# Gated DeltaNet and windowed attention, one core: the inverse's two upper levels by smaller blocks, and four steps put elsewhere

## The chip, the cores and the metric

One NeuronCore of a Trainium2 chip runs the whole program in one launch. Its engines are TensorE (PE; its weight loads are shown as PEld), VectorE (DVE), ScalarE (ACT), GpSimd (POOL) and SyncE (SP), which issues the weight loads from HBM. The metric is the device time of one execution in microseconds (us).

## The reference, cut to what matters

A prompt of 256 tokens and a decode batch of 8 go through a gated DeltaNet layer and a windowed attention layer, each followed by a SwiGLU block. The change touches the DeltaNet layer alone, where each head needs, for each chunk of tokens, the inverse of a lower triangular matrix:

```
a_mat = jnp.where(strict, jnp.einsum('bhnid,bhnjd->bhnij', kb, k) * decay, 0.0)
t_mat = lax.linalg.triangular_solve(a_mat + eye, jnp.broadcast_to(eye, a_mat.shape),
                                    left_side=True, lower=True)
u = t_mat @ (v * beta[..., None])
...
o = rms_norm(o, gnorm) * jax.nn.silu(z)
y = o.astype(h.dtype).reshape(B, L, DN_VAL_DIM) @ w_out
```

The kernel works with chunks of 128 tokens (the reference with 64), so each inverse is 128x128.

## The kernel before, in words

**Weights.** Every projection is done in chunks of 128x1024 weights. A chunk is loaded by SP, ACT rounds it (`split_hi`, line 460, `w_hi`), DVE makes the rest (`split_lo`, line 467, `w_lo`), and PE then runs 24 matmuls of 128x264 on it (`tiles`, lines 479 to 481: w_hi by h_hi, w_hi by h_lo, w_lo by h_hi). There are four buffers of raw weights and two of the split ones, so ACT may split chunk c only once PE is through with chunk c-2.

**Turns.** The DeltaNet layer's 32 heads come in 16 groups of two. `turn(g, G, last)` projects group g (12 chunks, j = 0 to 11) while group G = g-1 goes through its delta rule in 24 steps, n = 0 to 23: PE does step 2j, half of chunk j, step 2j+1, and the other half. So a step of PE comes once in some 2.2 us. ACT, DVE and POOL have their own parts of each step, in a hand written order around the splits. `first_turn` projects group 0 with no delta rule beside it; the last turn (g is None) takes the first 12 chunks of the output projection in place of a projection's.

**The inverse.** Four 128x128 matrices (two heads by two chunks, index m_) are inverted together by doubling: steps 4 to 8 make the inverses of small diagonal blocks, and then each level joins two neighbours, X = N12 U2 and then U1 X. Um holds the two 64x64 diagonal halves of each matrix (rows 0 to 63 and 64 to 127), Tm is Um transposed in 32x32 squares, Nm the matrix itself, UF the finished 128x128 inverse. UF shares its memory with NT, and the profile calls it NT. `each4` issues eight 64x64 matmuls: for each m_ one for the upper half and one for the lower half, in two different corners of the array. Steps 8 and 10 join 16 to 32, steps 11 and 12 join 32 to 64, both with `each4`; steps 13 and 14 join 64 to 128 with four 64x64 matmuls each, all in one corner (lines 1937 and 1943). Step 15 is the first user of UF. Each fp32 matmul has two records in the trace.

**What lies between them.** After step 10 DVE adds into Um (line 2251) and transposes it into Tm; after 11 it masks the product into Xm (2252, 128x256); after 12 it subtracts the halves into UF (2287, two of 64x256) and transposes a 32-row piece into Tm (2290), and only then splits the next chunk; after 13 it copies Xm (2293); after 14 ACT writes the last quarter of UF (1684).

**The other places.** In `first_turn` DVE does the convolution's taps 6 and 7 of v behind the split of the following turn's first chunk (line 467), at j = 11; ACT's `silu_v` (1638), a table load (1639) and `early(0, 22)` (1653 to 1658, the norm of q and k) come behind these taps, then DVE's product (2203), and on it waits PE's step 1 of group 0 (1876). At the start of the last turn ACT runs `tail_hi` (1663, rounding of the gated output) and then `unit_copy(G, 2, ...)` (1586, the gate z of the last group out of PSUM), on which PE waits in the middle of chunk 0. After the last turn ACT and DVE split chunk 13, finish the last group (`tail`, `tail_hi`), and then split chunk 14.

Of the kernel before, what the change touches and what calls it, by code (L numbers as in the profile page):

```python
# [14 lines left out]
HP = P // 2  # L15
EPS = 1e-6
# [39 lines left out]
def yoco_step(nc, x_prompt, x_sample, state_delta, state_conv, cache_k, cache_v, norm_mix, norm_ffn,  # L56
# [60 lines left out]
    with ctx:  # L117
# [555 lines left out]
        def act_after_delta(act):  # L673
# [49 lines left out]
            columns(C_OUT, UNIT["out"], 0, done=13)  # L723
# [768 lines left out]
        def _(act):  # L1492
# [172 lines left out]
            def step(G, n):  # L1665
# [13 lines left out]
                elif n == 7:  # L1679
                    act.wait_ge(inv_pe, 13 * G + 7)  # L1680
                    nc.scalar.activation(Nm[:, :, :], B[0][:, :], ACT.Copy).then_inc(inv_act, 1)
                elif n == 14:
                    act.wait_ge(inv_pe, 13 * G + 13)
                    nc.scalar.activation(UF[0:HP, :, HP:P], B[0][0:HP, 0:2 * P].rearrange("p (m n) -> p m n", m=4),
                                         ACT.Copy, scale=-1.0).then_inc(inv_act, 1)
# [23 lines left out]
            def turn(g, G, last, odd):  # L1709

                for j in range(12):
# [5 lines left out]
                    for n in (2 * j, 2 * j + 1):  # L1717
# [17 lines left out]
                        if n == 0 and last is not None:  # L1735
                            tail_hi(last)
                        if n == 0 and G is not None:
                            unit_copy(G, 2, 1 - odd)
# [34 lines left out]
            split_hi(act, chunk(C_OUT, RAW, 0, 13))  # L1773
            tail_hi(GROUPS - 1)
# [6 lines left out]
        def _(pe):  # L1781
# [64 lines left out]

            def each4(out, lhsT, rhs_):
# [22 lines left out]
            def step(G, n):  # L1870
                inv = lambda s, k: pe.wait_ge(s, (5 if s is inv_act else 15) * G + k)
# [55 lines left out]
                elif n == 11:  # L1927
                    inv(inv_dve, 10)
                    each4(B[0], full(Nm), half(Um)).then_inc(inv_pe, 1)
                elif n == 12:  # L1930
                    inv(inv_dve, 12)
                    each4(B[1], half(Tm), half(Xm)).then_inc(inv_pe, 1)
                elif n == 13:

                    inv(inv_dve, 13)
                    for m_ in range(4):
                        m = nc.tensor.matmul(B[3][block(0), m_ * HP:(m_ + 1) * HP], Nm[block(1), m_, block(0)],
                                             UF[block(1), m_, block(1)], start=True, stop=True)
                    m.then_inc(inv_pe, 1)
                elif n == 14:  # L1940
                    inv(inv_dve, 15)
                    for m_ in range(4):
                        m = nc.tensor.matmul(B[0][block(0), m_ * HP:(m_ + 1) * HP], Tm[block(0), m_, :],
                                             Xm[block(0), m_, :], start=True, stop=True)
                    m.then_inc(inv_pe, 1)
                elif n == 15:
                    inv(inv_act, 5)
# [148 lines left out]
        def _(dve):  # L2096
# [125 lines left out]
            def step(G, n):  # L2222
# [24 lines left out]
                elif 4 <= n <= 13 and n != 9:  # L2247
# [5 lines left out]
                    if n == 4:  # L2253
                        dve.wait_ge(inv_act, 5 * G + 1)
                        turned(PbT, Pb)
                    elif n == 5:
                        dve.wait_ge(inv_act, 5 * G + 2)
# [22 lines left out]
                    elif n == 11:  # L2280
                        got(10)
                        msk(0, lvl32_h)
                    elif n == 12:
                        got(11)
                        own(10)
                        for b in range(2):
                            m = tt(dg(UF, b), hm(Um, b), m4(B[1][HP * b:HP * (b + 1), 0:2 * P]), ALU.subtract)
                        m.then_inc(inv_dve, 1)
                        own(13)
                        nc.vector.transpose(Tm[32:64, :, 0:32], UF[0:32, :, 32:64]).then_inc(inv_dve, 1)  # L2290
                    elif n == 13:
                        got(12)
                        nc.vector.tensor_copy(hm(Xm, 0), m4(B[3][0:HP, 0:2 * P])).then_inc(inv_dve, 1)
# [54 lines left out]

            CONV = {16: (2, 3), 17: (4, 5), 18: (6,), 19: (7,)}

            def turn(g, G, last):

                for j in range(12):
                    for n in (2 * j, 2 * j + 1):
# [8 lines left out]
                        if g is not None:  # L2363
                            if 8 <= n < 14:
                                conv(g, 0, n - 6)
                            for k in CONV.get(n, ()):
                                conv(g, 1, k)
                            early(g, n)

            def first_turn():  # L2370

                split_lo(dve, first_chunk(4))
                for j in range(4, 12):
# [11 lines left out]
                    elif j == 10:  # L2385
                        write_gates(2)
                        for k in range(3, 6):
                            conv(0, 1, k)
                    else:
                        conv(0, 1, 6)  # L2390
# [295 lines left out]
```

## Time and profile before

| what | value |
|---|---|
| median of three runs | 2975.74 us (2975.68 to 2975.78) |
| the profiled execution | 2975.96 us, span 2974.2 us |
| PE busy | 2937.6 us, 99% |
| DVE busy | 1785.7 us, 60% |
| ACT busy | 1390.4 us, 47% |
| granted TensorE clock, mean | 0.994 |
| DMA engines | 57.5% of 16 engines' span |

The busy time of PE counts every matmul in flight, so it does not tell how fast they follow one another; the starts in the timeline do. "Idle before" is counted from the end of the one before, which is modelled.

### The profile page before, as it was taken

What the parts mean: (1) busy time and instruction counts of PE and PEld (TensorE: products, weight loads), DVE (VectorE), ACT (ScalarE), POOL (GpSimd) and SP (SyncE); (2) the same over time, 40 slices, a digit from 0 to 9 for tenths busy, and PEclk for the clock granted to TensorE, in tenths of its full rate; (3) what the DMA queues carried; (4) which work ended last, traced back from release to release, by engine and by line L of the source; (5) the groups of instructions that cost most, each with busy time, mean ns of one, the idle gap of its engine ahead of it and who ended that gap; (6) DMA issues with size and microseconds to landing.
All of it is one profiled execution on the core that took longest, in us unless ns stands there. A gap on an engine that the chain in (4) does not pass through costs nothing.

```text
span 2974.2 us, 68822 instructions
## 1 busy us (share of the span) xinstructions
PE 2937.6 (99%) x25560; PEld 2858.6 (96%) x25560; DVE 1785.7 (60%) x2807; ACT 1390.4 (47%) x2040; POOL 172.1 (6%) x268
## 2 busy tenths in 40 slices
PE   8999999999999999999999999999999999999999
PEld 7899999999999999999999999999999999999999
DVE  6777777778777545555555544576555555554444
ACT  5555556556555434444444333555444444444333
POOL 0212212211111000000000000000000000000000
PEclk9999999999999999999999999999999999999999
DMA  7565565655655665555555556744456565656654
GB/s 211 161 183 159 176 179 159 174 178 152 177 170 149 210 191 177 177 181 178 180 179 179 182 160 181 215 147 128 145 176 183 177 181 178 180 180 179 182 172 150
DMA packets 520519, 518.92 MB, mean 174 GB/s; under 512 B 31807, under 2 KB 443624, under 8 KB 520088
## 3 DMA queue, kind: packets, MB, share of 16 engines
q1 hardware_dynamic: 518574, 510.21, 57.5%
q0 software_dynamic: 1152, 5.58, 0.6%
q8 instruction: 152, 2.49, 0.4%
q14 instruction: 47, 0.39, 0.0%
q10 hardware_dynamic: 594, 0.25, 0.0%
HBM read 491.99 MB, written 32.82 MB: 176 GB/s over the span
## 4 chain that ended last, share of the span: by engine, by line
PE 67%; issue 0%; DVE 0%; ACT 0%; DVEq 0%; ACTq 0%
PE bank L479 22%; PE bank L481 21%; PE bank L480 21%; PE bank L1034 0%; PE bank L1010 0%; PE bank L1046 0%; PE bank L1022 0%; PE bank L1036 0%; PE bank L587 0%; PE bank L1147 0%; ACT w_hi L460 0%; PE bank L1069 0%; DVE w_lo L467 0%; PE bank L1011 0%; PE bank L1024 0%
## 5 line engine op out<-in xcount | busy, mean ns | idle before, releaser
L467 DVE TENSOR_TENSOR w_lo<-w_raw,w_hi 128x1024 fp32r<-128x1024 f32 x858 | 1049.1, 1223 | 959.4 <-ACT w_hi L460 957.4
L460 ACT ACTIVATE w_hi<-w_raw 128x1024 fp32r<-128x1024 f32 x858 | 908.6, 1059 | 1353.5 <-PE bank L481 1352.1
L479 PE MATMUL bank<-h_hi,w_hi 128*128 128x264 f32 x4624 | 1354.3, 293 | 7.6 <-DVE w_lo L467 7.0
L481 PE MATMUL bank<-h_hi,w_lo 128*128 128x264 f32 x4624 | 1315.5, 284 | 0.0
L480 PE MATMUL bank<-h_lo,w_hi 128*128 128x264 f32 x4624 | 1315.2, 284 | 0.0
L479 PEld LDWEIGHTS bank<-h_hi,w_hi 128*128 128x128 f32 x4624 | 873.3, 189 | 30.4 <-issue 11.2
L480 PEld LDWEIGHTS bank<-h_lo,w_hi 128*128 128x128 f32 x4624 | 875.2, 189 | 1.4
L481 PEld LDWEIGHTS bank<-h_hi,w_lo 128*128 128x128 f32 x4624 | 873.2, 189 | 0.0
L479 PE MATMUL bank<-a_hi,w_hi 128*128 128x264 f32 x1408 | 401.2, 285 | 8.5 <-issue 6.2
L480 PE MATMUL bank<-a_lo,w_hi 128*128 128x264 f32 x1408 | 402.0, 286 | 0.0
L481 PE MATMUL bank<-a_hi,w_lo 128*128 128x264 f32 x1408 | 401.3, 285 | 0.0
L479 PEld LDWEIGHTS bank<-a_hi,w_hi 128*128 128x128 f32 x1408 | 265.8, 189 | 9.1 <-issue 8.9
L480 PEld LDWEIGHTS bank<-a_lo,w_hi 128*128 128x128 f32 x1408 | 265.8, 189 | 0.0
L481 PEld LDWEIGHTS bank<-a_hi,w_lo 128*128 128x128 f32 x1408 | 265.6, 189 | 0.0
L479 PE MATMUL bank<-o_hi,w_hi 128*128 128x264 f32 x512 | 148.2, 289 | 1.6 <-DVE w_lo L467 0.9
L481 PE MATMUL bank<-o_hi,w_lo 128*128 128x264 f32 x512 | 145.6, 284 | 0.0
L480 PE MATMUL bank<-o_lo,w_hi 128*128 128x264 f32 x512 | 145.4, 284 | 0.0
L2182 DVE SCALAR_TENSOR_TENSOR cacc<-craw,convw,cacc 128x256 f32<-128x256 f32 (+1 forms) x192 | 103.6, 562 | 5.3 <-ACT cacc L1605 3.3
L479 PEld LDWEIGHTS bank<-o_hi,w_hi 128*128 128x128 f32 x512 | 96.4, 188 | 3.3 <-DVE w_lo L467 1.2
L480 PEld LDWEIGHTS bank<-o_lo,w_hi 128*128 128x128 f32 x512 | 96.7, 189 | 0.1
L481 PEld LDWEIGHTS bank<-o_hi,w_lo 128*128 128x128 f32 x512 | 96.6, 189 | 0.0
L479 PE MATMUL bank<-ao_hi,w_hi 128*128 128x264 f32 x320 | 92.8, 290 | 0.0
(375 smaller groups left out, 2667.8 us busy)
## 6 DMA issues: line engine op xcount, KB each, us to landing
w_raw<-in_w_gate_up_dram SPq DMA_DIRECT2D x704, 256.0 KB, 2.9
w_raw<-in_w_in_a_dram SPq DMA_DIRECT2D x388, 256.0 KB, 3.1
w_raw<-in_w_down_dram SPq DMA_DIRECT2D x352, 256.0 KB, 3.1
w_raw<-in_w_out_a_dram SPq DMA_DIRECT2D x128, 256.0 KB, 3.3
s_dec<-in_state_delta_dram SPq DMA_DIRECT2D x32, 512.0 KB, 5.5
out_dram<-s_dec SPq DMA_DIRECT2D x32, 512.0 KB, 5.0
w_raw<-in_w_q_b_dram SPq DMA_DIRECT2D x64, 256.0 KB, 3.0
w_raw<-in_w_o_b_dram SPq DMA_DIRECT2D x64, 256.0 KB, 3.0
```

Of the source, the lines that this page charges most:

```text
L460: nc.scalar.activation(w_hi[:, s % SPL, :], w_raw[:, s, :], ACT.Copy).then_inc(hi_ready, 1)
L467: ops.tensor_tensor(w_lo[:, s % SPL, :], w_raw[:, s, :], w_hi[:, s % SPL, :].bitcast(F32), ALU.subtract).then_inc(lo_ready, 1)
L479: nc.tensor.matmul(bank[bk][:, 0:T], wh, xh, start=first, stop=False)
L480: nc.tensor.matmul(bank[bk][:, 0:T], wh, xl, start=False, stop=False)
L481: m = nc.tensor.matmul(bank[bk][:, 0:T], wl, xh, start=False, stop=last)
L2182: stt(cacc[:, t, 0:n], craw[:, t, j:j + n], convw[:, ds(g, 1), t, j], cacc[:, t, 0:n], ALU.mult, ALU.add).then_inc(conv_out if k == 7 else ...
```

## The change

It has five parts.

1. **Steps 11 and 12** work on 32x32 blocks: eight 32x32 matmuls with 32 columns each, in place of eight 64x64. Since only the 32x32 off-diagonal part is made, ACT copies Um into the diagonal blocks of UF (a new step 11, two instructions, waits for DVE), DVE copies 96x128 into Xm without a mask, and writes two 32x128 pieces of UF with a factor of -1 in place of the two subtractions.
2. **Steps 13 and 14** put matrices 2 and 3 into PSUM rows 64 to 127, beside 0 and 1, so that two 64x64 matmuls lie in two corners. For that ACT copies half of Tm to rows 64 to 127 (a new step 12), DVE makes two small transposes, the copy into Xm is 128x128, and ACT writes the last quarter of UF by two instructions. PE's step 13 waits for ACT's new step 11, its step 14 and DVE's second transposes for ACT's new step 12.
3. **DVE's order.** The transposes for step 14 move from step 12, ahead of the split of chunk 7, to step 13, behind it; taps and exponents' differences that stood at step 12 move to step 13.
4. **First group:** taps 6 and 7 of v move from j = 11 to j = 10, ahead of the split.
5. **End:** in the last turn ACT copies the gate ahead of `tail_hi`; chunk 14's split goes ahead of `tail_hi` on ACT and ahead of the second part of `tail` on DVE.

```diff
+                elif n == 11:
+                    act.wait_ge(inv_dve, 15 * G + 10)
+                    for b in range(2):
+                        at = slice(HP * b, HP * (b + 1))
+                        m = nc.scalar.activation(UF[at, :, at], Um[at, :, :], ACT.Copy)
+                    m.then_inc(inv_act, 1)
+                elif n == 12:
+                    act.wait_ge(inv_pe, 13 * G + 11)
+                    nc.scalar.activation(Tm[HP:P, 2:4, :], Tm[0:HP, 2:4, :], ACT.Copy).then_inc(inv_act, 1)
                 elif n == 14:
                     act.wait_ge(inv_pe, 13 * G + 13)
-                    nc.scalar.activation(UF[0:HP, :, HP:P], B[0][0:HP, 0:2 * P].rearrange("p (m n) -> p m n", m=4),
-                                         ACT.Copy, scale=-1.0).then_inc(inv_act, 1)
+                    for b in range(2):
+                        m = nc.scalar.activation(UF[0:HP, 2 * b:2 * b + 2, HP:P],
+                                                 B[0][HP * b:HP * (b + 1), 0:P].rearrange("p (m n) -> p m n", m=2),
+                                                 ACT.Copy, scale=-1.0)
+                    m.then_inc(inv_act, 1)
...
-                        if n == 0 and last is not None:
+                        if n == 0 and g is None:
+                            unit_copy(G, 2, 1 - odd)
                             tail_hi(last)
-                        if n == 0 and G is not None:
-                            unit_copy(G, 2, 1 - odd)
+                        elif n == 0:
+                            if last is not None:
+                                tail_hi(last)
+                            if G is not None:
+                                unit_copy(G, 2, 1 - odd)
...
             split_hi(act, chunk(C_OUT, RAW, 0, 13))
+            split_hi(act, chunk(C_OUT, RAW, 0, 14))
             tail_hi(GROUPS - 1)
...
                 elif n == 11:
                     inv(inv_dve, 10)
-                    each4(B[0], full(Nm), half(Um)).then_inc(inv_pe, 1)
+                    for m_ in range(4):
+                        for b in range(2):
+                            lo, up = quarter(b, 1), quarter(b, 0)
+                            m = nc.tensor.matmul(B[0][up, m_ * QP:(m_ + 1) * QP], Nm[lo, m_, up],
+                                                 Um[lo, m_, QP:2 * QP], start=True, stop=True)
+                    m.then_inc(inv_pe, 1)
                 elif n == 12:
                     inv(inv_dve, 12)
-                    each4(B[1], half(Tm), half(Xm)).then_inc(inv_pe, 1)
+                    for m_ in range(4):
+                        for b in range(2):
+                            up = quarter(b, 0)
+                            m = nc.tensor.matmul(B[1][up, m_ * QP:(m_ + 1) * QP], Tm[up, m_, 0:QP], Xm[up, m_, 0:QP],
+                                                 start=True, stop=True)
+                    m.then_inc(inv_pe, 1)
                 elif n == 13:
+                    inv(inv_act, 5)
                     inv(inv_dve, 13)
-                    for m_ in range(4):
-                        m = nc.tensor.matmul(B[3][block(0), m_ * HP:(m_ + 1) * HP], Nm[block(1), m_, block(0)],
-                                             UF[block(1), m_, block(1)], start=True, stop=True)
+                    for i in range(2):
+                        for b in range(2):
+                            m_ = 2 * b + i
+                            m = nc.tensor.matmul(B[3][block(b), i * HP:(i + 1) * HP], Nm[block(1), m_, block(0)],
+                                                 UF[block(1), m_, block(1)], start=True, stop=True)
                     m.then_inc(inv_pe, 1)
                 elif n == 14:
+                    inv(inv_act, 6)
                     inv(inv_dve, 15)
-                    for m_ in range(4):
-                        m = nc.tensor.matmul(B[0][block(0), m_ * HP:(m_ + 1) * HP], Tm[block(0), m_, :],
-                                             Xm[block(0), m_, :], start=True, stop=True)
+                    for i in range(2):
+                        for b in range(2):
+                            m = nc.tensor.matmul(B[0][block(b), i * HP:(i + 1) * HP], Tm[block(b), 2 * b + i, :],
+                                                 Xm[block(b), i, :], start=True, stop=True)
                     m.then_inc(inv_pe, 1)
...
                     elif n == 11:
                         got(10)
-                        msk(0, lvl32_h)
+                        nc.vector.tensor_copy(Xm[0:96, :, 0:QP], m4(B[0][0:96, 0:P])).then_inc(inv_dve, 1)
                     elif n == 12:
                         got(11)
-                        own(10)
+                        dve.wait_ge(inv_act, 7 * G + 5)
                         for b in range(2):
-                            m = tt(dg(UF, b), hm(Um, b), m4(B[1][HP * b:HP * (b + 1), 0:2 * P]), ALU.subtract)
+                            at = HP * b
+                            m = ts(UF[at:at + QP, :, at + QP:at + HP], m4(B[1][at:at + QP, 0:P]), -1.0, None, ALU.mult)
                         m.then_inc(inv_dve, 1)
+                    elif n == 13:
                         own(13)
-                        nc.vector.transpose(Tm[32:64, :, 0:32], UF[0:32, :, 32:64]).then_inc(inv_dve, 1)
-                    elif n == 13:
+                        dve.wait_ge(inv_act, 7 * G + 6)
+                        for b in range(2):
+                            at = HP * b + QP
+                            m = nc.vector.transpose(Tm[at:at + QP, 2 * b:2 * b + 2, 0:QP],
+                                                    UF[0:QP, 2 * b:2 * b + 2, QP:HP])
+                        m.then_inc(inv_dve, 1)
                         got(12)
-                        nc.vector.tensor_copy(hm(Xm, 0), m4(B[3][0:HP, 0:2 * P])).then_inc(inv_dve, 1)
+                        nc.vector.tensor_copy(Xm[:, 0:2, :], B[3][:, 0:P].rearrange("p (m n) -> p m n", m=2)
+                                              ).then_inc(inv_dve, 1)
...
+            CONV_QK = {8: (2,), 9: (3,), 10: (4,), 11: (5,), 13: (6, 7)}
...
-                            if 8 <= n < 14:
-                                conv(g, 0, n - 6)
+                            for k in CONV_QK.get(n, ()):
+                                conv(g, 0, k)
...
-                            early(g, n)
+                            for m in {12: (), 13: (12, 13)}.get(n, (n,)):
+                                early(g, m)
...
                     elif j == 10:
                         write_gates(2)
-                        for k in range(3, 6):
+                        for k in range(3, 8):
                             conv(0, 1, k)
                     else:
-                        conv(0, 1, 6)
-                        conv(0, 1, 7)
...
             split_lo(dve, chunk(C_OUT, RAW, 0, 13))
             tail(GROUPS - 1, 0)
+            split_lo(dve, chunk(C_OUT, RAW, 0, 14))
             tail(GROUPS - 1, 1)
```

The counts of ACT's semaphore go from 5 to 7 a group, and the output projection's later loops start at chunk 14 in place of 13.

## Rows read from the trace of the kernel before

**Rows 1.** The page's part 1: busy time, share and instructions of PE.

```profile
PE 2937.6 (99%) x25560; PEld 2858.6 (96%) x25560; DVE 1785.7 (60%) x2807; ACT 1390.4 (47%) x2040; POOL 172.1 (6%) x268
```

**Rows 2.** Waits of PE, whole span: waiter, releaser, us in total, times, longest.

```profile
PE bank L479 <- DVE w_lo L467: 7.9, 18, 1.3
...
PE bank L479 <- ACT zs L1586: 0.7, 1, 0.7
```

**Rows 3.** PE's timeline, steps 11 and 13: start, us, instruction, shapes, count.

```profile
434.66 0.28 PE L480 MATMUL bank<-h_lo,w_hi 128*128 128x264 f32 x1
434.79 0.28 PE L481 MATMUL bank<-h_hi,w_lo 128*128 128x264 f32 x1
434.99 0.68 PE L1851 MATMUL bank<-Um,Nm 64*64 64x64 f32 x16
435.61 0.39 PE L479 MATMUL bank<-h_hi,w_hi 128*128 128x264 f32 x1
...
439.52 0.68 PE L1937 MATMUL bank<-NT,Nm 64*64 64x64 f32 x8
440.13 0.39 PE L479 MATMUL bank<-h_hi,w_hi 128*128 128x264 f32 x1
```

**Rows 4.** PE's timeline in the attention layer: 16 pairs with 4 moving columns.

```profile
1988.48 1.10 PE L1069 MATMUL bank<-pdT,v_win 128*64 128x4 f32 x32
```

**Rows 5.** Single lines: duration in ns min/median/max, first and last start, shapes.

```profile
L1069 PE MATMUL bank<-pdT,v_win x128: 199/199/221, 1988.5 to 2104.1; 128*64 128x4 f32 x128
L1069 PEld LDWEIGHTS bank<-pdT,v_win x128: 132/138/138, 1988.5 to 2104.0; 128*64 128x64 f32 x128
L1978 PEld LDWEIGHTS bank<-s_dec,kq_diag x256: 106/110/110, 117.4 to 948.6; 128*32 128x32 f32 x128
L1046 PEld LDWEIGHTS bank<-q_dec,k_t x64: 183/188/188, 1966.7 to 2088.3; 64*128 64x128 f32 x64
```

**Rows 6.** Timelines of DVE and ACT behind steps 11, 12, 13 and 14.

```profile
435.98 0.42 DVE L2252 TENSOR_TENSOR Xm<-bank,masks 128x256 f32<-128x256 f32 x1
...
437.99 0.85 DVE L2287 TENSOR_TENSOR NT<-Um,bank 64x256 f32<-64x256 f32 x2 [1.00 <-PE bank L1851]
...
441.07 0.42 DVE L2293 COPY Xm<-bank 64x256 f32<-64x256 f32 x1
...
442.85 0.36 ACT L1684 ACTIVATE NT<-bank 64x256 f32<-64x256 f32 x1
```

**Rows 7.** Timeline of group 0's start, and a stretch's busy times and clock.

```profile
72.32 1.23 DVE L467 TENSOR_TENSOR w_lo<-w_raw,w_hi 128x1024 fp32r<-128x1024 f32 x1 [0.97 <-ACT w_hi L460]
73.46 0.89 DVE L2182 SCALAR_TENSOR_TENSOR cacc<-craw,convw,cacc 128x264 f32<-128x264 f32 x2
...
74.39 0.65 ACT L1638 ACTIVATE cacc<-cacc 128x528 f32<-128x528 f32 x1 [2.10 <-DVE cacc L2182]
...
76.35 0.85 ACT L1653 ACTIVATE qk_sq<-bank,bias_c 128x264 f32<-128x264 f32 x2
...
78.86 1.59 PE L1876 MATMUL bank<-qk 128*128 128x256 f32 x4 [3.06 <-DVE qk L2203]
...
79.39:82.80 3.41, 3.41 (x15) 3.07 (x14) 3.36 (x5) 2.10 (x5) 2.52 (x5) 0.50 0.80 231
```

**Rows 8.** Timelines of DVE and ACT at the start of the last turn.

```profile
910.87 0.71 DVE L2216 TENSOR_TENSOR norm_h<-norm_h,zs 128x528 f32<-128x528 f32 x1
...
912.17 0.65 ACT L1586 ACTIVATE zs<-bank 128x264 f32<-128x264 f32 x2
```

**Rows 9.** Timelines of ACT and PE at chunk 14 of the output projection.

```profile
969.10 1.05 ACT L460 ACTIVATE w_hi<-w_raw 128x1024 fp32r<-128x1024 f32 x1
...
971.46 0.39 PE L479 MATMUL bank<-o_hi,w_hi 128*128 128x264 f32 x1 [0.94 <-DVE w_lo L467]
```

**Rows 10.** Two later places: a stretch at half clock, and PE's wait in the last block.

```profile
2007.90:2011.31 3.41, 3.41 (x20) 0.50 0.86 258
...
2831.17 0.38 PE L479 MATMUL bank<-a_hi,w_hi 128*128 128x264 f32 x1 [2.31 <-DVE x_res L2409]
```

More of the change, by code:

```diff
@@ L15 @@
 HP = P // 2
+QP = P // 4
 EPS = 1e-6
@@ L721, in ffn @@
                 columns(C_DOWN[l], UNIT["down"], 2 * l + 1, last=l == 1)
-            columns(C_OUT, UNIT["out"], 0, done=13)
+            columns(C_OUT, UNIT["out"], 0, done=14)
             ffn(0)
@@ L1845, in block, with quarter @@
                 return slice(HP * b, HP * (b + 1))
+            def quarter(b, half_):
+                at = HP * b + QP * half_
+                return slice(at, at + QP)
             def each4(out, lhsT, rhs_):
@@ L1870, in step @@
             def step(G, n):
-                inv = lambda s, k: pe.wait_ge(s, (5 if s is inv_act else 15) * G + k)
+                inv = lambda s, k: pe.wait_ge(s, (7 if s is inv_act else 15) * G + k)
                 if n == 1:
@@ L1945, in step @@
                     m.then_inc(inv_pe, 1)
                 elif n == 15:
-                    inv(inv_act, 5)
+                    inv(inv_act, 7)
                     for h in range(2):
@@ L2253, in step @@
                     if n == 4:
-                        dve.wait_ge(inv_act, 5 * G + 1)
+                        dve.wait_ge(inv_act, 7 * G + 1)
                         turned(PbT, Pb)
                     elif n == 5:
-                        dve.wait_ge(inv_act, 5 * G + 2)
+                        dve.wait_ge(inv_act, 7 * G + 2)
                         turned(PaT, Pa)
@@ L2499, in _ @@
             nc.vector.memset(dec_sel[:, 1, :], 0.0).then_inc(u_read, 1)
-            add_columns(C_OUT, UNIT["out"], 0, done=13)
+            add_columns(C_OUT, UNIT["out"], 0, done=14)
             ffn(0)
```

## The prediction

> **What bounds the kernel now.** I read the page first. PE is busy in 99% of the span [rows 1]: nothing else can bound the whole, so only two kinds of edit can pay, those that take time out of PE's own stream and those that end a wait of PE. Next the waits of PE [rows 2]: it waits little, 7.9 us for w_lo in 18 places and 0.7 us once for the gate z; the longest wait that the change aims at is 3.06 us, for the product that makes q and k of group 0 [rows 7]. Then PE's timeline around the steps of the inverse, by starts and not by busy time. Within a chunk a 128x264 matmul follows the last after 0.12 to 0.13 us (434.66 to 434.79). At step 11 the last of the chunk starts at 434.79, the block at 434.99, and the chunk goes on at 435.61: 0.82 us in place of 0.12, so step 11 costs 0.70 us. Of this 0.20 us lie before the block and 0.62 us from its start to the chunk's going on. Step 13 has half as many records (8 against 16) and takes the same 0.61 us, 439.52 to 440.13 [rows 3]. So two 64x64 matmuls in two corners cost what one costs alone: time goes by intervals, eight in each block. An interval is (1.10 - 0.20) / 15 = 60 ns for 16 pairs with 64 weight columns [rows 4, 5]; for step 11 itself (0.68 - 0.2) / 7 is a little more, since its first interval is longer [rows 3].
>
> **Steps 13 and 14, paired.** Four matmuls in one corner have eight intervals; two by two they have four. 4 x 0.060 less some 0.01 us within a pair is 0.23 us a block. Pairs exist in before with the same row half and two column halves (rows 4 has 32 records in the time of 16 intervals), which is step 13's form, and as diagonal corners (step 11), which is step 14's. Two blocks in 16 groups: 32 x 0.23 = **7.4 us**.
>
> **Steps 11 and 12, 32x32.** Still eight intervals, only narrower; no row has a matmul with 32 weight columns and 32 moving ones. One bound is nothing: in rows 4 four moving columns in place of 64 don't make the interval shorter than 60 ns, so what sets it is either the weight load or a floor. The other is by the weight loads: 188 ns with 128 columns, 132 to 138 with 64, 106 to 110 with 32 [rows 5]: from 64 to 32 they fall by 26 ns, just as steeply as from 128 to 64. If the interval follows them it is 34 ns, and a block saves 8 x 0.026 = 0.21 us; 32 blocks, **6.7 us**. I take this, since the 32-column load is the row nearest to the new shape. The 0.20 us ahead of the block stay.
>
> In this trace pairs start together and 60 ns part pairs of 64 columns [rows 4, 5]. The Trainium skill ("TensorE: Matmul & The Clock Gate", section "Wait — 56ns, not 53.3ns?") says that matmuls never start closer than about 25 ns however few their columns. With 25 ns for each record (an estimate from that page) a pair would take 50 ns, and steps 11 and 12 would save 2.6 us and not 6.7. No row here shows such a matmul.
>
> **What the new steps cost on other engines.** ACT's step 11 (two copies of 64x256) and 12 (one of 64x128), nearest row 0.36 us each [rows 6], come where ACT sits idle, and nothing is queued behind but chunk 7's and 8's splits, which wait for PE anyway. DVE's copy for step 12 is no longer than 0.42 us (435.98), the two pieces of UF are smaller than the two subtractions (0.85 us for both). For step 13 PE needs these pieces: after step 12 DVE began at 437.99; 0.6 to 0.85 us later is 438.8 at most, and PE's step came at 439.52. For step 14 PE needs the transposes and Xm: the split (1.23 us) follows the pieces and ends near 440.1 at most; two small transposes (an estimate, 0.2 us each, from the 0.42 of copies four times their size) and the copy (0.42 at most) end near 440.9, against 441.49 before (441.07 + 0.42) and PE's step 14 at about 441.4, half a chunk and a step (12 x 0.122 + 0.7) after step 13's 439.52, less the 0.3 us by which PE is ahead. ACT's last quarter becomes two instructions, at most 0.36 us more behind 442.85; PE's step 15 comes at about 443.9, 0.7 us after its end. So all is covered, by 0.4 us at the tightest; if the cover were gone, see the rivals. The waits for w_lo in rows 2 at a turn's third chunk come of DVE's queue over the turn's end, which starts from PE's last steps and moves with it: they stay, 0 us. That chunk 7's split is earlier gains nothing by itself.
>
> **First group.** DVE's two taps (73.46, 0.89 us) stand behind a split at 72.32, which waited 0.97 us for ACT's rounding of the same chunk; the taps fit into this wait. ACT's silu of v then starts not at 74.39 but when its rounding has ended, 72.3; the 1.96 us from its start to ACT's next (74.39 to 76.35) put that at 74.3. What is late next is PE's sum of squares, which ended half a chunk before PE's wait began: 78.86 - 3.06 - 12 x 0.122 = 74.3. So ACT's next (76.35 before) starts at 74.4, 1.95 us earlier, and with it PE's step 1, at 76.9 and not 78.86 [rows 7]. Its wait of 3.06 us shrinks to 1.1. Behind the wait the granted clock was 0.50 (the lower of its two levels, 1.2 GHz) from 79.39 to 82.80 [rows 7]; PE's other waits for DVE, up to 1.3 us [rows 2], had none behind them. I count this stretch as gone: half of 3.41, 1.7 us. About 0.1 us come back as a wait for the third chunk, as other groups have it: 1.95 + 1.7 - 0.1 = **3.6 us**; bounds 1.9 and 3.7.
>
> **Gate.** The copy of z began at 912.17 and took 0.65. It can't start before DVE's gating, which ends at 911.58 (910.87 + 0.71) and still reads the old z, so it gains 0.55 of the 0.7 us. `tail_hi` comes later by 0.5 us on ACT, and DVE's rounding behind it delays the third chunk's split by 0.1 to 0.2 us, where nothing covers it [rows 2, 8]: **0.4 us**.
>
> **Last split.** ACT's split of chunk 14 began at 969.10, behind `tail_hi`; its buffer is free once chunk 12 is done, 24 x 0.122 = 2.9 us before PE's arrival at chunk 14 (971.46 - 0.94 = 970.5), so at 967.6. DVE then ends it at 970.0, before 970.5. The wait of 0.94 us goes [rows 9]. Group 15's rounding ends 0.7 us later, at 970.6; chunk 15, which needs it, comes at 973.4. **0.9 us**.
>
> **Sum.** 7.4 + 6.7 + 3.6 + 0.4 + 0.9 = 19.0 us.
>
> **What the shift may cost.** PE's clock fell also in the attention layer (0.50 from 2007.90 to 2011.31), without a wait, and did not fall at the wait of 2.31 us before 2831.17 [rows 10], though this wait is near the 3.06 us that had half clock behind it. All these places come 15 to 19 us earlier now, and whether the clock falls there may change: each fall costs up to 1.7 us (half of 3.41). Bounds: one fall less, -1.7, two more, +3.4. I take one more, 1.7 us, at the wait of 2.31: 19.0 - 1.7 = 17.3. From the profiled execution's 2975.96 this is 2958.7; the median of the runs is 0.2 below it, so **2958.4 us**.
>
> **Rivals.**
> - *A floor under the interval.* Four moving columns gave the same 60 ns as 64 would [rows 4], so a floor may be what rows 4 shows, and 32x32 blocks gain 0 to 2.6 us of the 6.7. For it: no interval in before is shorter than 60 ns. Against: the weight loads go on falling [rows 5]. It gives 2962.5 to 2965.1.
> - *A new wait takes the place.* The chain of step 12, UF pieces, step 13, transposes, step 14 passes between three engines, and with shorter steps PE asks 0.2 us sooner each time. If my cover of 0.4 us is too large by 0.8, each of 16 turns waits 0.4 us: 6.4 us back, 2964.8. Against: DVE and ACT are 60% and 47% busy [rows 1], and DVE waited 1.00 us before 437.99 [rows 6].
> - *Slower: small blocks each pay the change of form.* Between 128-wide and 64-wide matmuls PE spends 0.20 us in place of 0.12 at the start [rows 3], 0.08 us more. If 32x32 matmuls had to be set apart like this one by one, 32 blocks x 8 matmuls = 256 would cost 20 us and leave 2975.7 - 12.3 + 1.7 + 20 = 2985. It decides from about 41 ns each (10.6 / 256). Against: pairs of 64x64 pay it once a block.
> - *The first group keeps its half clock:* 1.7 us back, 2960.1; within the forecast's own range.
>
> **How the numbers follow.** Forecast 0.50, its own range 2955 to 2961. Floor 0.32, new wait 0.12, slower 0.03, and 0.03 that most of it is lost in something not seen. The range reaches from 2955 (forecast with one fall of the clock less) to 2966 (no gain at all from steps 11 and 12, with the extra fall), and holds the second rival. A measurement of this kernel can tell about 0.2%, 6 us, from no change; 2969.8 is that limit. Faster 0.92, same 0.05, slower 0.03.
>
> **What would show it.** In the trace of after: step 13's 8 records in 0.45 us and not 0.68; steps 11 and 12's 16 records in 0.47 if I am right, 0.6 or more with a floor; PE's step 1 of group 0 near 76.9 with a wait of 1.1 and clock 1.00 behind it; no waits of PE at 912 over 0.2 and at 971 over 0.1; each turn shorter by 0.88 us. The prediction is wrong if waits for ACT or DVE appear at steps 13 to 15 in every turn, or if a turn is shorter by less than 0.4 us.

## The result, and the profile after

The kernel after takes **2950.96 us** (median of four runs, 2950.39 to 2952.57), the kernel before 2975.71 beside it: ratio 0.9918, interval 0.9901 to 0.9936. The time fell by 24.7 us, where 17.3 was forecast, and lies below the forecast's range of 2955 to 2966.

The page's part 1 of after answers to [rows 1]: the same instructions of PE, 20.2 us less busy.

```profile
PE 2917.4 (99%) x25560; PEld 2839.8 (96%) x25560; DVE 1780.6 (60%) x2823; ACT 1410.9 (48%) x2104; POOL 172.0 (6%) x268
```

PE's timeline of after at steps 11 and 14 (start, us, instruction, shapes, count) answers to [rows 3]:

```profile
425.30 0.28 PE L482 MATMUL bank<-h_hi,w_lo 128*128 128x264 f32 x1
425.51 0.44 PE L1957 MATMUL bank<-Um,Nm 32*32 32x32 f32 x16
425.88 0.39 PE L480 MATMUL bank<-h_hi,w_hi 128*128 128x264 f32 x1
...
431.37 0.28 PE L482 MATMUL bank<-h_hi,w_lo 128*128 128x264 f32 x1
431.58 0.45 PE L1983 MATMUL bank<-Xm,Tm 64*64 64x64 f32 x8
431.95 0.39 PE L480 MATMUL bank<-h_hi,w_hi 128*128 128x264 f32 x1
```

From the block's start to the chunk's going on it is 0.37 us and not 0.62. Over all groups the medians are 612 to 370 ns for steps 11 and 12, 605 to 378 for 13 and 14. PE waits in neither place. A turn, from one group's step 1 to the next one's, fell from 55.35 to 54.39 us (medians).

Waits of PE in after (waiter, releaser, us in total, times, longest) answer to [rows 2, 7 and 10]:

```profile
PE bank L480 <- DVE w_lo L468: 9.6, 18, 2.6
...
PE bank L480 <- DVE x_res L2457: 2.2, 1, 2.2
...
PE bank L1900 <- DVE qk L2243: 1.5, 1, 1.5
...
PE bank L480 <- ACT zs L1587: 0.2, 1, 0.2
```

The wait for q and k is halved, that for the gate fell from 0.7, and that for chunk 14's w_lo is gone. The longest in the first row, 2.6 us, is a place that the prediction doesn't name. It lies in the first SwiGLU block's down projection, which PE runs as a loop of two passes (`pe.Fori(0, 2)` in `columns`), after 1056 of its 2112 matmuls, so where the loop goes back for its second pass. PE's timeline there, first before, then after:

```profile
1762.92 0.28 PE L481 MATMUL bank<-a_hi,w_lo 128*128 128x264 f32 x1
1769.40 0.58 PE L479 MATMUL bank<-a_hi,w_hi 128*128 128x264 f32 x1 [6.21 <-issue]
```

```profile
1742.90 0.28 PE L482 MATMUL bank<-a_hi,w_lo 128*128 128x264 f32 x1
1745.80 0.38 PE L480 MATMUL bank<-a_hi,w_hi 128*128 128x264 f32 x1 [2.62 <-DVE w_lo L468]
```

The DMA queue that carries instructions, in the time of each wait (packets, MB, share of 16 engines), again before and after:

```profile
q8 instruction: 2, 0.03, 1.9%
```

```profile
q8 instruction: 1, 0.02, 2.2%
```

In before two fetches of 16 KB lie in the wait, at 1763.14 and 1766.89, in after one, at 1743.18. PE goes on 2.5 and 2.6 us behind the start of the last one, 1.5 and 1.7 us behind its end. The wait of 2.31 us before 2831.17, which the prediction reads in [rows 10], is the same place in the second SwiGLU block: one fetch, and PE goes on 1.8 us behind its end.

**Where the 25.2 us of the two profiled executions went**, read as the shift between the same matmuls of the two traces:

| place | forecast | measured | how read |
|---|---|---|---|
| steps 13, 14 | 7.4 | 7.3 | 32 x 0.227 |
| steps 11, 12 | 6.7 | 7.7 | 32 x 0.242 |
| first group | 3.6 | 3.1 | wait 3.06 to 1.53; no half clock behind it, 1.58 |
| gate | 0.4 | 0.3 | 0.69 to 0.24, and 0.14 later |
| last split | 0.9 | 0.9 | wait of 0.94 gone |
| start of the program | 0 | 0.8 | half clock for 6.8 us, not 10.2 |
| sum up to here | 19.0 | 20.35 | shift in the output projection; the lines above give 20.1 |
| behind it, until 1207 | 0 | -0.3 | given back |
| jump back in the first down projection | 0 | 3.4 | 6.21 to 2.62, and the clock behind |
| attention layer | 0 | 1.8 | two stretches of half clock for three |
| wait of 2.31 in the second block | -1.7 | 0 | no half clock behind it in either |

The 0.8 us at the program's start are not the change's: k13_ahead (below), whose PE program is the one of before until the delta rule is done, has a stretch of 6.8 us there too.

### The profile page after: what moved, and what is told of

Its sections match the earlier page's. It is cut to its first block, busy times and chain, and to the rows that moved or that the text cites. A ratio compares the mean times of both kernels' runs of the same rounds, so it can differ in the third digit from the quotient of the medians.

```text
span 2949.0 us, 68978 instructions
## 1 busy us (share of the span) xinstructions
PE 2917.4 (99%) x25560; PEld 2839.8 (96%) x25560; DVE 1780.6 (60%) x2823; ACT 1410.9 (48%) x2104; POOL 172.0 (6%) x268
## 4 chain that ended last, share of the span: by engine, by line
PE 68%; DVE 0%; issue 0%; ACT 0%; DVEq 0%; ACTq 0%
PE bank L480 22%; PE bank L482 22%; PE bank L481 22%; PE bank L1035 0%; PE bank L1011 0%; PE bank L1047 0%; PE bank L1023 0%; PE bank L1037 0%; PE bank L588 0%; PE bank L1148 0%; PE bank L1070 0%; PE bank L1012 0%; PE bank L1025 0%; DVE w_lo L468 0%; DVE x_res L2457 0%
```

## The experiments

Each is told against the kernel before on the same chip.

**One half of the change each.** k1_places is the kernel before with parts 4 and 5 alone; k2_inverse is the kernel after without them.

> The kernel before with parts 4 and 5 alone (first group's last taps, last gate, last split); the inverse as before, PE's program unchanged. By the steps of the prediction, with the first group's wait as the trace of the changed kernel has it: 1.4 us of the wait, 1.7 us of half clock behind it, 0.4 for the gate, 0.9 for the split, less 0.1: 4.3 us by the end of the output projection's start. Theory 'code': the wait near 1769 stays 6.2 us, total about 2971.5, give or take 1.8 for one clock fall in the attention layer more or less. Theory 'time': the wait changes, since PE comes 4 us sooner.

> The changed kernel without parts 4 and 5: the inverse's four steps and DVE's order alone. Intervals: 32 blocks by 0.24 us (32x32) and 32 by 0.225 us (pairs) make 14.9 us over the 16 groups; a turn is 0.95 us shorter; the wait of 3.06 us in the first group with its half clock, 0.7 at the gate and 0.9 at chunk 14 stay. Theory 'code': the wait behind the loop near 1769 is 2.6 us, another 3.4 to 3.6 us: 2957. Theory 'time': between 2957 and 2961. The rival that the parts help each other would show as a turn of another length than in the changed kernel (54.40).

k1_places took 2970.59 us, ratio 0.9983 (0.9974 to 0.9993). PE's first step 1:

```profile
76.09 0.48 PE L1881 MATMUL bank<-qk 128*128 128x256 f32 x1 [1.53 <-DVE qk L2208]
```

The turn that follows takes 55.07 us in place of 56.65, the other turns 55.34 as before, the gate's wait is 0.24 us, chunk 14's is gone, and PE's wait at the jump back is still 6.18 us, with two fetches. One wait is new, at the next chunk, 15. DVE's timeline there, then PE's:

```profile
972.67 1.45 DVE L2413 TENSOR_TENSOR x_res<-x_res,bank 128x264 f32<-128x264 f32 x4 [1.59 <-DMA x_res<-x_spill]
```

```profile
975.30 0.39 PE L479 MATMUL bank<-o_hi,w_hi 128*128 128x264 f32 x1 [0.76 <-DVE w_lo L467]
```

The split of w_lo stands behind this addition to x_res, for which DVE waited 1.59 us until a DMA landed. In after DVE waits 0.84 us and PE not at all, in k7_long 1.39 and PE 0.6, so what the last split brings is not the same in every kernel.

k2_inverse took 2955.37 us, ratio 0.9931 (0.9914 to 0.9947), with turns of 54.39 us, the old waits of 3.06, 0.71 and 0.95 us, and 2.81 us at the jump back. The times alone give 5 us to the three moves and 20 to the inverse, but they hold more than that. By the shift in the output projection, less that of the program's start, the moves bring 3.8 us and the inverse 15.2. Of the rest, k2_inverse has 3.2 us from the jump back, and both have 1.5 to 1.8 us from the attention layer, where they have two stretches of half clock for three. The shorter wait at the jump back belongs to the inverse's half, which alone changes PE's stream of instructions.

**The wait where the loop goes back.** k3_waits is the kernel before with two waits more in each group on PE, both on a count that ACT reached long before; nothing else is changed.

```diff
                 elif n == 13:
+                    inv(inv_act, 4)
                     inv(inv_dve, 13)
...
                 elif n == 14:
+                    inv(inv_act, 4)
                     inv(inv_dve, 15)
```

> The kernel before, with two more waits per group in PE's program (steps 13 and 14), on a count of ACT's that step 8 has already waited for, so they hold nothing up: PE's program is as long as in the changed kernel, 32 instructions longer than before, and nothing else is changed. Theory 'code': PE's wait of 6.2 us near 1769 (behind a loop's end, with two instruction fetches of 16 KB in it) falls to 2.6 us as in the changed kernel, since it hangs on where the program's pieces lie; total near 2972.4, 3.4 us less. Theory 'time': the wait hangs on when PE comes there; here it comes at the same time as before, so 6.2 us and 2975.9 stay.

It took 2970.27 us, ratio 0.998 (0.997 to 0.9989), with the turns of before, 55.34 us. Of the 5.3 us, 3.3 are the shift at this wait and 1.6 a stretch of half clock less in the attention layer. k13_ahead puts the 32 waits in one place, behind the last turn:

```diff
             turn(None, GROUPS - 1)
+            for _ in range(32):
+                pe.wait_ge(inv_act, 5 * GROUPS)
             pe_after_delta(pe)
```

> The kernel before with 32 waits of TensorE, all on a count reached long before, in one place behind the last turn and ahead of the loops that follow; the groups are untouched. Theory (the wait behind the loop is set by where the stream stands in the fetched pieces): as in k3_waits, where the same number of waits was spread over the groups, one fetch lies in the wait and it is 2.4 to 3.0 us, not 6.2; the turns are 55.35 us. Rival (in k3_waits the waits inside the groups changed something else): 6.2 us with two fetches.

PE's timeline there, k3_waits and then k13_ahead:

```profile
1762.47 0.28 PE L481 MATMUL bank<-a_hi,w_lo 128*128 128x264 f32 x1
1765.41 0.54 PE L479 MATMUL bank<-a_hi,w_hi 128*128 128x264 f32 x1 [2.67 <-DVE w_lo L467]
```

```profile
1762.55 0.28 PE L481 MATMUL bank<-a_hi,w_lo 128*128 128x264 f32 x1
1765.99 0.58 PE L479 MATMUL bank<-a_hi,w_hi 128*128 128x264 f32 x1 [3.17 <-DVE w_lo L467]
```

One fetch lies in each, and 32 instructions without work take 3.0 to 3.5 us off the wait (3.17 is a little above what I expected). k13_ahead's single time was 2972.16 us; its granted clock was 0.50 for 6.8 us from 1765.08, so that the shift at this wait is only 1.8 us. To see whether the position repeats, k7_long puts 14 waits more a group into the kernel after, which makes 256 with the change's own 32:

```diff
                 elif n == 14:
                     inv(inv_act, 6)
                     inv(inv_dve, 15)
+                    for _ in range(14):
+                        inv(inv_act, 5)
```

> The kernel after with 14 more waits a group on TensorE's stream at step 14, all on a count that VectorE or ScalarE reached before: nothing to compute, 224 more instructions in the unrolled groups (256 with the 32 that the change itself brings, against the kernel before). Theory (TensorE's wait behind the end of the loop is a fetch of instructions, and how long it is follows from where in a fetched piece the stream stands, not from the work): the wait near 1746 us, 2.6 in the kernel after, takes another length, 6.2 us if the piece's bounds fall as they did before, and whatever it becomes shows in the total; the turns of the loop that hold the waits too are longer by at most 0.1 us each. Rival (the long wait belongs to the 64x64 blocks or to DMA traffic of the kernel before): it stays at 2.6 us. Each wait costs a few ns at most, so the total is 2951 to 2952 with a short wait and 2954.5 to 2955.5 with the long one.

The wait was 2.94 us, with one fetch, the turns 54.39, the time 2951.79 us, ratio 0.9915 (0.9898 to 0.9931). My guess of the position fell: 256 instructions more don't bring the long wait back. What stands is that before and k1_places, whose PE streams are the same, have 6.2 us and two fetches, and all twelve kernels with another stream, after among them, 2.1 to 3.5 us. Which positions are the bad ones stays open.

That the fetch ends the wait, and not the split that the profile names, can be read in all fourteen kernels. In both down projections PE goes on 1.5 to 1.8 us behind the end of the last fetch before it, 28 times of 28. In k10_late (below) PE doesn't wait for that split at all: it starts at 1714.41, and the split ends at 1714.96. PE's line, then DVE's:

```profile
1714.41 0.38 PE L482 MATMUL bank<-a_hi,w_hi 128*128 128x264 f32 x1 [2.08 <-DVE x_res L2464]
```

```profile
1713.74 1.22 DVE L470 TENSOR_TENSOR w_lo<-w_raw,w_hi 128x1024 fp32r<-128x1024 f32 x1
```

**Small blocks and pairs apart.** k5_small keeps the 32x32 blocks of steps 11 and 12 and has steps 13 and 14 as before; k6_pairs is the reverse.

> The kernel after with the blocks of 32x32 at steps 11 and 12 kept and steps 13 and 14 as in the kernel before (no pairs). Theory (the two halves of the inverse's change are independent and each is its count of blocks by what a block is shorter): a turn of about 54.87 us, that is 54.39 and two blocks of 0.24 us given back; over 15.5 turns 7.4 us above the kernel after, so about 2958.4 us. Rival (the blocks share a limit, so that one half alone brings nearly all): a turn under 54.6 us. Rival (the pairs bring nearly all, the small blocks little): a turn above 55.1 us.

> The kernel after with the pairs at steps 13 and 14 kept and steps 11 and 12 by 64x64 blocks as in the kernel before. Theory (independent halves): a turn of about 54.87 us (two blocks of 0.24 us given back), about 2958.4 us. If both this kernel and the one with the small blocks alone stand at 54.87, the saving is per block and adds up; if either stands within 0.1 of 54.39 or of 55.34, it doesn't.

k5_small: a turn of 54.84 us, 2959.76 us, ratio 0.9945 (0.9928 to 0.9961). k6_pairs: 54.89 us, 2960.22 us, ratio 0.9949 (0.9932 to 0.9965). From 55.35 they take 0.51 and 0.46 off a turn, 0.97 together, and the whole change takes 0.96: the two add, and the small blocks are worth a little more than the pairs, not less.

**VectorE's order.** k4_order is the kernel after with DVE's second transposes at step 12, ahead of chunk 7's split, where the kernel before had them, and the tap and the difference of step 12 back there.

```diff
                         m.then_inc(inv_dve, 1)
-                    elif n == 13:
                         own(13)
                         dve.wait_ge(inv_act, 7 * G + 6)
...
                         m.then_inc(inv_dve, 1)
+                    elif n == 13:
                         got(12)
```

> The changed kernel with DVE's old order: the second transposes at step 12, ahead of chunk 7's split, and taps and exponents at step 12 again. They now wait for ACT's copy of Tm, which stands behind ACT's split of chunk 7. My theory: the cover is wide either way, PE has no new wait, 2951 within 0.3 us, all turns 54.4. Rival: DVE held at step 12 delays w_lo of chunk 7 or Xm, and PE waits at step 13 or chunk 7 in each turn, 0.1 to 0.5 us by 15 turns, 2952.5 to 2958.

It took 2955.72 us (2951.49 to 2956.22), ratio 0.9926 (0.991 to 0.9943), 4.8 us above the kernel after. The two intervals overlap, but the turns don't leave it open: 54.73 us for 54.39, 5.1 us over 15 turns. Waits of PE, then DVE's timeline, both of k4_order:

```profile
PE bank L1983 <- DVE Xm L2339: 4.4, 15, 0.4
```

```profile
430.10 0.58 DVE L2328 TENSOR_SCALAR NT<-bank 32x128 f32<-32x128 f32 x2 [0.73 <-PE bank L1965]
431.11 0.49 DVE L2334 STREAM_TRANSPOSE Tm<-NT 32x64 f32<-32x64 f32 x2 [0.43 <-ACT Tm L1692]
431.63 1.23 DVE L468 TENSOR_TENSOR w_lo<-w_raw,w_hi 128x1024 fp32r<-128x1024 f32 x1
...
433.49 0.29 DVE L2339 COPY Xm<-bank 128x128 f32<-128x128 f32 x1
```

DVE waits 0.43 us for ACT's new copy of Tm, which stands behind a rounding of 1.06 us on ACT; the transposes and then the split come later by that, and Xm, behind two taps, is late for PE's step 14 by 0.3 to 0.4 us in 15 turns. In after the split fills that time:

```profile
428.11 0.58 DVE L2328 TENSOR_SCALAR NT<-bank 32x128 f32<-32x128 f32 x2 [0.76 <-PE bank L1965]
428.79 1.23 DVE L468 TENSOR_TENSOR w_lo<-w_raw,w_hi 128x1024 fp32r<-128x1024 f32 x1
430.05 0.49 DVE L2335 STREAM_TRANSPOSE Tm<-NT 32x64 f32<-32x64 f32 x2
430.56 0.29 DVE L2339 COPY Xm<-bank 128x128 f32<-128x128 f32 x1
```

**The first group's last 0.4 us.** DVE's timeline of after, at the five taps that now stand in a row:

```profile
69.19 0.20 DVE L2209 SCALAR_TENSOR_TENSOR tab_eb<-tab_eb 128x32 f32<-128x32 f32 x1
69.30 2.86 DVE L2222 SCALAR_TENSOR_TENSOR cacc<-craw,convw,cacc 128x256 f32<-128x256 f32 x5
72.09 1.21 DVE L468 TENSOR_TENSOR w_lo<-w_raw,w_hi 128x1024 fp32r<-128x1024 f32 x1
```

They take 2.86 us, and not the 1.27 and 0.89 that they took in two places before. The fourth alone takes 1.27 (70.49 to 71.76), and beside it runs GpSimd's product:

```profile
70.31 1.17 POOL L1414 TENSOR_TENSOR NT<-masks,sc_b 128x512 f32<-128x512 f32 x1
```

k11_taps puts the taps ahead of the gate tables that start this product:

```diff
                     elif j == 10:
-                        write_gates(2)
                         for k in range(3, 8):
                             conv(0, 1, k)
+                        write_gates(2)
```

> The kernel after with one thing moved in the first group: VectorE's last five taps ahead of the gate tables (write_gates) in place of behind them, so that GpSimd's product, which starts off these tables, runs behind the taps and not beside them. Theory (the tap of 1.27 us, where others of its size take 0.48, was held by GpSimd's product): all five taps take 0.40 to 0.48 us, silu of v starts 0.5 to 0.7 us earlier relative to the chunk's rounding, and the wait of TensorE's first step 1 falls from 1.53 to 0.9 us. Rival (the long tap has another cause, its size or its place): a tap of 1.2 us stays and the wait is at least 1.5. The total moves by 0.6 us at most, which only the profile can show.

DVE and the first wait in k11_taps:

```profile
69.08 2.08 DVE L2222 SCALAR_TENSOR_TENSOR cacc<-craw,convw,cacc 128x256 f32<-128x256 f32 x5
```

```profile
76.07 1.13 PE L1900 MATMUL bank<-qk 128*128 128x256 f32 x4 [1.09 <-DVE qk L2243]
```

Every tap takes 0.48 us, and the wait is 1.09: the figure of the prediction, once nothing holds the tap. The time was 2949.2 us, ratio 0.9917 (0.9902 to 0.9932), which can't be told from the kernel after.

**Further down the same road.** In k9_quarters the levels 8 to 16, 16 to 32 and 32 to 64 are held as strips of 32x32 blocks, and `each4` puts four of them side by side:

```diff
-                    for b in range(2):
-                        mm = nc.tensor.matmul(out[block(b), m_ * HP:(m_ + 1) * HP], lhsT(m_, b), rhs_(m_, b),
-                                              start=True, stop=True)
+                    for b in range(4):
+                        mm = nc.tensor.matmul(out[QP * b:QP * (b + 1), m_ * QP:(m_ + 1) * QP], lhsT(m_, b), rhs_(m_, b),
+                                              start=True, stop=True, tile_position=(QP * b, QP * b))
```

> The kernel after with the two middle levels of the inverse, 8 to 16 and 16 to 32, and the level 32 to 64 held as strips of 32x32 blocks: every step from the strips computes four corner blocks of 32x32 side by side on TensorE in place of one 64x64 or 128x128 record. Eight blocks a turn change. Theory (what made a record cheap in the change is its size, and four records in different corners of the array run beside one another at about 32 ns a round, as the pairs did): each of them is some 0.2 us shorter, 1.6 us a turn, about 2924 us. Rival (four records in one round are bound by their issue, some 16 ns each, 64 ns a round, which is what a 64x64 record took): no gain, 2951 to 2953. Second rival (the other engines' work at the start of the turn, the copies in four pieces, comes due too early): new waits of 0.1 to 0.3 us a turn in front of the second step of the inverse, which take 2 to 5 us of the gain.

It took 2931.36 us (2930.4 to 2932.36), ratio 0.985 (0.9833 to 0.9866). PE's timeline at a step with two blocks (64 records), and at the start of the same turn:

```profile
404.24 0.45 PE L1877 MATMUL bank<-Pb,PbT 32*32 32x32 f32 x32
404.51 0.48 PE L1877 MATMUL bank<-Um,Pb 32*32 32x32 f32 x32
404.92 0.39 PE L482 MATMUL bank<-h_hi,w_hi 128*128 128x264 f32 x1
```

```profile
402.59 0.39 PE L482 MATMUL bank<-h_hi,w_hi 128*128 128x264 f32 x1 [0.67 <-DVE w_lo L470]
```

The step takes 0.68 us in place of 1.08 with 32 records of 64x64, a single block 0.38 in place of 0.61: eight blocks are 1.7 us a turn. But the turn fell by only 1.23, for the second rival held at a higher price than I gave it: the wait at the third chunk, 0.27 us in after, is 0.67, where I had expected 0.1 to 0.3. The masking of PaT is four instructions on DVE, and the split behind it is late. DVE's timeline, a turn later:

```profile
452.09 1.17 DVE L2282 TENSOR_TENSOR PaT<-NT,masks 32x128 f32<-32x128 f32 x4
453.30 0.31 DVE L2285 STREAM_TRANSPOSE Pa<-PaT 128x128 f32<-128x128 f32 x1
453.53 0.65 DVE L2287 TENSOR_TENSOR intraT<-bank,intraT 128x512 f32<-128x512 f32 x1
454.11 0.41 DVE L2291 TENSOR_TENSOR qdec<-qk,egR 128x256 f32<-128x256 f32 x1
454.44 1.22 DVE L470 TENSOR_TENSOR w_lo<-w_raw,w_hi 128x1024 fp32r<-128x1024 f32 x1
```

intraT and qdec have no user for many steps. k10_late puts them behind the split (`elif n == 3:` ahead of these two products in DVE's `step`, nothing else).

> The kernel with 32x32 blocks in every level but the last, and VectorE's two products that nobody waits for soon (the masked scores and the decayed q of the group) put behind the split of chunk 2 in place of ahead of it. In the trace of k9_quarters TensorE waits 0.68 us once a turn for this split, which starts 1.06 us too late behind those two products. Theory (that wait is the only thing that the small blocks cost): it goes, a turn is 52.5 us, and the kernel takes about 2921 us. Rival (the products are then late for what comes next on VectorE, the transpose at step 5, or on TensorE): a new wait of 0.2 to 0.5 us a turn, 2924 to 2929.

It took **2918.95 us** (2918.33 to 2920.91), ratio 0.9813 (0.9799 to 0.9826), a turn of 52.33 by the median. Two of the 15 turns are longer, by waits of 0.4 and 1.0 us marked as issue that end 2.4 and 2.6 us behind the start of a fetch. The wait of 0.67 us at the third chunk is gone, and with it the 0.27 of after. Together with the 1.7 that makes 2.0, against 54.39 - 52.33 = 2.06. Waits of PE:

```profile
PE bank L482 <- DVE w_lo L470: 3.8, 4, 1.4
```

k12_both is k10_late with the taps of k11_taps.

> The kernel with 32x32 blocks in every level but the last (k10_late) and the first group's five taps ahead of the gate tables (k11_taps). Both gains are on TensorE's path and in different places, so they should add: the wait at the first step 1 is 1.1 us in place of 1.53, the turns stay at 52.45 us, and the total is 0.4 us under that of k10_late, 2918.5 us, a difference that the profile can show and the times can't. Rival (VectorE's split, which now runs beside GpSimd's product, is late for the first turn): a new wait of 0.2 to 0.8 us there.

It took 2919.25 us (2917.39 to 2920.61), ratio 0.9811 (0.9798 to 0.9825): the first wait is 1.08 us, and the times can't tell this kernel from k10_late. These are the best kernels of this study, 32 us under the kernel after.

## Why the prediction was right and wrong

- **What bounds it, and counting intervals by starts:** right. A block of either kind became shorter by what it was to lose or a little more, and k5_small and k6_pairs show that the two halves add up.
- **Steps 13 and 14:** right, 0.227 us a block for 0.23.
- **Steps 11 and 12:** the mechanism held, a narrower weight load is a shorter interval; the term was too small. I took 34 ns from the line through 188, 135 and 108; pairs start 31.7 ns apart (425.565, 425.597, 425.628), and a block saved 0.24 and not 0.21. That is 1.0 us of the miss. The load of 32 columns takes 108 ns and that of 64 takes 134, so the interval (60 to 31.7) fell by about as much as the load.
- **The rival with a floor (0.32):** fell. Sixteen records in 0.44 us with the last 0.19 long leave (0.44 - 0.19) / 15 = 17 ns from start to start. The Trainium skill ("TensorE: Matmul & The Clock Gate", section "Wait — 56ns, not 53.3ns?") gives about 25 ns as the least distance of two starts. The trace disagrees for records in different corners: in a pair they start 7 ns apart, and k9_quarters has 64 in 0.68 us. Before could have told it, for its pairs in [rows 4] start 7 ns apart too (1988.478, 1988.485). From one pair to the next it is 32 ns, which doesn't contradict the page.
- **New waits (0.12):** none in after, so right in its result and wrong in one reason. "That chunk 7's split is earlier gains nothing by itself" failed: k4_order shows that the order is what keeps 5 us. I had checked DVE's time for the transposes and not what they wait for, ACT's new copy behind a rounding. The wait at a turn's third chunk stayed at 0.27 us, as forecast; k10_late shows that it can be had, by moving two products of DVE behind the split.
- **First group:** 3.1 us for 3.6. The wait is 1.53 and not 1.1, since I took five taps at their free time; k11_taps shows GpSimd's product as the cause. The half clock behind the wait went, as counted; it is there in the four kernels that have the wait of 3.06 us and in none of the ten with 1.1 to 1.5. That step 1 starts at 76.67, so near the 76.9 of the forecast, is luck: 0.64 us of it is the shift from the program's start.
- **Gate and last split:** 0.3 and 0.9 us for 0.4 and 0.9. Right.
- **"What the shift may cost":** failed, and with 3.5 us it is the largest part of the miss. I charged one more stretch at half clock, 1.7 us, at the wait of 2.31 us; after has none there and one less in the attention layer, worth 1.8. The attention layer has three such stretches in before and two in each of the other thirteen kernels, k3_waits and k13_ahead among them, which compute what before does. One lies behind the wait of 2.0 to 2.5 us in the second block in k6_pairs, k10_late, k11_taps and k12_both, and none in after or in before at 2.2 and 2.3. No row of before tells which it will be, so it should have stood in the range alone, on both sides.
- **The wait of 6.21 us at 1769:** overlooked, so put at nothing without a reason. It is PE's longest in before, it is marked as issue, and an edit that adds instructions to PE's stream can change it. k3_waits shows 3.5 us off the wait for that alone. Of the terms that the sum doesn't have it is the largest, 3.4 us. That it came out as a gain is luck too: nothing in the change was made for it.
- **The range:** its low end, 2955, was the sum with one stretch of half clock fewer than in before, and that much came in this term. What took the result out of the range are the others. With 1.0 for the interval, 3.4 for the jump back and 0.8 at the program's start it would have been near 2950.

Forecast to result in one line: 17.3 + 1.0 (interval) + 3.5 (clock, attention) + 3.4 (jump back) + 0.8 (start) - 0.7 (first group, gate and pairs) - 0.1 (the rest) = 25.2 us.

## What to carry to other kernels

In this kernel small fp32 matmuls cost by the width of the weights they load and by how many lie side by side, so cut a block of 64 into 32x32 corners where the other engines can take the pieces, and look behind it for the split or copy that has become late. Before an order on one engine is called indifferent, read for each moved instruction what it waits for on the others. And go through every long wait of the bounding engine, those marked as issue too: here 32 instructions without work took 3.5 us off one, nearly as much as three careful moves gained.

## What the runs showed of the hardware

- **Four corners at once.** In k9_quarters 32x32 matmuls in four corners start 7 ns apart and the next four 32 ns behind the first: the same interval as for the pairs of after, with twice the work in it.
- **Instruction fetch.** Where the down projection's loop goes back, PE waited 2.1 to 3.5 us in the first block when the last fetch of 16 KB was the only one to start in the wait or just ahead of it, and 6.2 with two. It went on 1.5 to 1.8 us behind the end of the last one, in both blocks of all fourteen kernels, whatever the profile names. 32 instructions more ahead of the loop, spread over the groups or in one place, took 6.2 us to 2.7 and 3.2.
- **VectorE beside GpSimd.** A tap of 128x264 takes 486 ns alone and 1272 to 1527 when it starts behind a GpSimd product, in 16 places of after, and each time it ends 0.29 to 0.30 us behind the product. In 15 places of after a split of the weights starts first, 0.2 to 0.5 us ahead of the product, and takes 1.21 us, no more than the 1.22 of all splits. In k11_taps, where the two start together at 71.52, it is GpSimd's small copy that stretches, from 0.27 to 1.27 us. The Trainium skill ("SBUF — State Buffer", section "SBUF: two separate sides") has the rule that fits: the two engines share a pair of ports under an exclusive lock, and whichever starts first holds it for its whole instruction. The trace agrees: the tap began at 70.49, 0.18 us behind GpSimd's product, and ended 0.29 us behind it.
